# Head pairs on two PSUM banks, taps moved forward, squares added before the token sums, and x turned unscaled in a hybrid layer with attention and experts

## The reference, cut to what matters

```python
h = rms_norm(x, g_mix[i]); proj = h @ w_in[i]              # conv value, conv gate, q, k, v
conv_out = conformer_conv(c_val, c_gate, ...)              # 31 causal taps on 512 channels, LayerNorm, silu
attn = moba_attention(q, k, to_heads(v))                   # 8 heads of 64; at 512 tokens: causal over everything
mixed = concatenate([rms_norm(conv_out, beta_conv), rms_norm(attn, beta_attn)])
x = x + mixed @ w_out[i]
h = rms_norm(x, g_ffn[i])
g_logits = h @ w_group + b_group; e_all = h @ w_erouter + b_erouter   # 4 + 32 logits of each token
# top group, then its top 2 of 8 experts; the chosen experts' SwiGLU on each token, weighted
x = x + hier_moe(h, ...)
x = x + (p[i] @ w_ple_proj) * sigmoid(rms_norm(x, g_ple) @ w_ple_gate + b_ple_gate)
```

## Time and profile before

| | |
|---|---|
| median of 3 runs | 652.24 us |
| the profiled execution's own time | 651.7 us |
| its span | 649.8 us |
| PE busy | 551.8 us (85%) |
| DVE busy | 297.3 us (46%) |
| ACT busy | 185.7 us (29%) |
| POOL busy | 82.2 us (13%) |
| chain that ended last | PE 55%, DVE 19%, DMA 15%, ACT 7% |

### The profile page before, as it was taken

One profiled execution on the slowest core, in us unless ns is written; L12 is line 12 of the kernel. 1 busy time (PEld: TensorE's weight loads), 2 busy tenths in 40 slices (PEclk: granted clock), 3 DMA queues, 4 the chain that ended last, 5 costly groups with the idle time before them and its releaser, 6 DMA issues.

```text
span 649.8 us, 7753 instructions
## 1 busy us (share of the span) xinstructions
PE 551.8 (85%) x2628; PEld 322.9 (50%) x2629; DVE 297.3 (46%) x551; ACT 185.7 (29%) x348; POOL 82.2 (13%) x106
## 2 busy tenths in 40 slices
PE   1999999985779898897997889999999998729980
PEld 1788887753456687543332233333333332228870
DVE  3339868998872924474211111211121121175754
ACT  4831411346742432121101010110111010154554
POOL 0650000000000030002112012112211211000000
PEclk9999999996779989989999899999999999958995
DMA  8902102545004001664899998699899999265012
GB/s 342 384 3 72 67 9 58 219 144 211 1 0 195 1 1 66 266 283 168 323 418 419 421 421 348 235 419 385 335 417 422 368 421 419 119 259 210 2 43 86
DMA packets 34248, 145.86 MB, mean 224 GB/s; under 512 B 6576, under 2 KB 6832, under 8 KB 21808
## 3 DMA queue, kind: packets, MB, share of 16 engines
q1 hardware_dynamic: 27168, 133.70, 51.6%
q0 software_dynamic: 6480, 10.50, 4.4%
q10 hardware_dynamic: 576, 1.34, 0.5%
HBM read 142.90 MB, written 14.68 MB: 242 GB/s over the span
## 4 chain that ended last, share of the span: by engine, by line
PE 55%; DVE 19%; DMA 15%; ACT 7%; issue 2%; SPq 1%; POOL 0%; DVEq 0%; ACTq 0%; POOLq 0%
PE bank L1518 17%; DMA wring<-w_up_in 12%; PE bank L1266 10%; PE bank L1534 7%; DVE mix L888 6%; PE bank L1379 6%; PE bank L1563 2%; PE bank L1290 2%; DVE wring L946 2%; PE bank L1360 1%; PE bank L1497 1%; DMA c<-cst_in 1%; PE bank L1347 1%; PE bank L1444 1%; PE bank L1314 1%
## 5 line engine op out<-in xcount | busy, mean ns | idle before, releaser
L1518 PE MATMUL bank<-wring,arena 128*64 128x512 f32 x640 | 142.8, 599 | 13.7 <-SPq L506 12.0
L1518 PEld LDWEIGHTS bank<-wring,arena 128*64 128x64 f32 x640 | 46.2, 138 | 107.4 <-issue 90.1
L888 DVE SCALAR_TENSOR_TENSOR mix<-arena,pr,mix 128x512 f32<-128x512 f32 x120 | 81.5, 751 | 0.0
L1534 PE MATMUL bank<-wring,arena 128*64 128x512 f32 x320 | 73.1, 599 | 9.5 <-ACT arena L800 9.5
L1176 DVE TENSOR_TENSOR arena<-arena,bank 128x256 f32<-128x256 f32 x20 | 8.4, 422 | 148.7 <-ACT arena L797 148.7
L797 ACT ACTIVATE arena<-bank 128x256 f32<-128x256 f32 x20 | 7.7, 384 | 143.9 <-PE bank L1518 143.9
L1534 PEld LDWEIGHTS bank<-wring,arena 128*64 128x64 f32 x320 | 21.2, 136 | 48.5 <-issue 34.3
L1181 DVE COPY arena<-bank 128x512 f32<-128x512 f32 x20 | 13.8, 692 | 66.4 <-PE bank L1534 66.4
L1266 PE MATMUL bank<-hT_hi,win_hi 128*128 128x512 f32 x128 | 33.5, 398 | 1.5 <-DVE hT_lo L866 0.9
L803 ACT ACTIVATE arena<-bank 128x512 f32<-128x512 f32 x20 | 11.9, 597 | 75.8 <-PE bank L1534 75.8
L1266 PE MATMUL bank<-hT_lo,win_hi 128*128 128x512 f32 x128 | 31.6, 389 | 0.0
(11 more groups left out here) (203 smaller groups left out, 812.0 us busy)
## 6 DMA issues: line engine op xcount, KB each, us to landing
wring<-w_gate_in SPq DMA_DIRECT2D x32, 1024.0 KB, 10.4
wring<-w_up_in SPq DMA_DIRECT2D x32, 1024.0 KB, 12.7
wring<-w_down_in SPq DMA_DIRECT2D x32, 1024.0 KB, 15.6
wring<-w_in_in SPq DMA_DIRECT2D x5, 2048.0 KB, 19.1
wring<-w_out_in SPq DMA_DIRECT2D x2, 2048.0 KB, 8.0
wring<-y_d SPq DMA_DIRECT2D x8, 512.0 KB, 6.8
xs<-x_in SPq DMA_DIRECT2D x4, 512.0 KB, 7.5
xs<-x_in SPq DMA_DIRECT2D x1, 2048.0 KB, 8.0
```

Of the source, the lines that this page charges most:

```text
L888: ins = dve.scalar_tensor_tensor(out=mixc[:, mm, :], in0=u[:, mm, j:j + S], scalar=w, in1=mixc[:, mm, :], op0=ALU.mult, op1=ALU.add)
L1518: ins = pe.matmul(pb[2 + s][a * CAP:(a + 1) * CAP, :], xgT[:, s, k, a * CAP:(a + 1) * CAP], up_w(w, a)[:, :, k, :], start=(k == 0), stop=( ...
L1534: ins = pe.matmul(pb[6 + half][a * CAP:(a + 1) * CAP, :], hidT[:, s, k, a * CAP:(a + 1) * CAP], dn_w(w, a)[:, k, half * 512:(half + 1) * 5 ...
```

## The change

- **Banks.** Pairs of heads alternate between banks 6 and 7. "outa" uses five banks in turn and "outc" three; "h2" uses four; mean, var and the sums of squares move to banks 4 and 5.
- **Taps.** 71 in place of 66 taps stand before the attention, 13 of them ahead of the first turn of the rotation where 10 stood behind it; then seven each for four units, and one for each unit after that (two before). 13 are left after the last unit (6 before).
- **ACT.** probs_out goes ahead of attn_out, and the split of w_out's convolution half goes behind the loop.
- **Squares.** POOL adds the four tiles of the attention's squares, DVE those of the convolution; PE sums the one tile by token. The mean is made after the third "outa" group (before: second), conv_sq after the second "outc" group (before: first).
- **Router.** x is turned as it is, without the root. The gains are multiplied into wr once, on DVE. The logits are made with tokens on partitions, one tile after the other, and DVE multiplies by the root and adds a row of the bias, which was stored to memory and read back to all partitions by two small DMAs on SP's queue. ACT copies out one half of each turned tile, DVE the other. The rows' scaling for the gather remains, and for the last tile it stands in the middle of the router's chain on DVE. The DMA of wpp is issued ahead of the last "outc" group.

```diff
-GLU2, GLU3, TURN, EARLY = 20, 34, 54, 66
-TAPS_BY = (73, 80, 87, 94) + tuple(range(96, 120, 2))
+GLU2, GLU3, TURN, EARLY = 20, 34, 57, 71
+TAPS_BY = (78, 85, 92, 99) + tuple(range(100, 112))
...
-            banks.use(("attn", u // TT), 6)
-    banks.use("attn_sq", 7)
+            banks.use(("attn", u // TT), 6 + u // TT % 2)
+    banks.use("attn_sq", 4)
     for q in range(2 * TT):
-        banks.use(("outa", q), q % 4)
-    banks.use("mean", 4)
-    banks.use("var", 5)
+        banks.use(("outa", q), (0, 1, 2, 6, 7, 0, 1, 2)[q])
+    banks.use("mean", 5)
+    banks.use("var", 4)
     for q in range(2 * TT):
-        banks.use(("outc", q), q % 4)
-    banks.use("conv_sq", 7)
+        banks.use(("outc", q), q % 3)
+    banks.use("conv_sq", 5)
...
+            sp.wait_ge(prm_loaded, 32)
+            sp.dma_start(bias_d, pr[0:NR, Q_RB:Q_RB + 1]).then_inc(rbias_stored, 16)
             banks.wait_full(sp, ("v", TT - 1))
...
+            banks.wait_full(sp, ("outa", 2 * TT - 1))
+            sp.dma_start(wpp, ...).then_inc(ple_loaded, 16)
+            sp.wait_ge(rbias_stored, 16)
+            sp.wait_ge(osq_ready, CM)
+            sp.dma_start(bias_row, bias_d.rearrange("n a -> (a n)").partition_broadcast(P)).then_inc(rbias_loaded, 16)
             banks.wait_full(sp, ("outc", 2 * TT - 1))
-            sp.dma_start(wpp, ...).then_inc(ple_loaded, 16)
             sp.dma_start(pTs, ...).then_inc(ple_loaded, 16)
...
+            for m in range(CM):                          # POOL
+                banks.wait_emptied(pool, ("attn", m))
+                split_mix(1, mixa, m)
+                if m >= 1:
+                    pool.wait_ge(sqa_ready, m + 1)
+                    wait(pool, sq_added, m - 1)
+                    pool.tensor_tensor(sqa[:, 0, :], sqa[:, 0, :], sqa[:, m, :], ALU.add).then_inc(sq_added, 1)
...
-                if 9 <= u_ < 9 + CM:                     # ACT
-                    split_out(0, u_ - 9)
+                if u_ >= 2:
+                    probs_out(u_ - 2)
                 if u_ % TT == 3 and u_ > TT:
                     attn_out(u_ // TT - 1)
-                if u_ >= 2:
-                    probs_out(u_ - 2)
             attn_out(CM - 1)
+            act.wait_ge(woc_loaded, 16)
+            for m in range(CM):
+                split_out(0, m)
+            banks.wait_full(act, "attn_sq")
+            emptied(act.activation(gss[:, 1, :], bk("attn_sq")[:, 0:TT], ACT.Sqrt, ...), "attn_sq")
...
                 mean_root(1, t, junk)
+                banks.wait_full(act, ("h2", t, 1))
+                emptied(act.activation(hT[:, 4:8, t * P:(t + 1) * P], ..., ACT.Copy), ("h2", t, 1))
...
-            taps(GLU3 - 6, TURN - 10)                    # DVE
+            taps(GLU3 - 6, TURN)
             turn(0)
-            taps(TURN - 10, TURN)
+            dve.tensor_tensor(wr[:], wr[:], pr[:, Q_FFN:Q_FFN + DK]..., ALU.mult).then_inc(wr_scaled, 1)
             taps(TURN, EARLY)
...
-            for q in range(2):
+            for q in range(3):
                 add_scaled(("outa", q), 1, q)
...
+            for m in range(1, CM):
+                dve.wait_ge(osq_ready, m + 1)
+                wait(dve, csq_added, m - 1)
+                dve.tensor_tensor(sqc[:, 0, :], sqc[:, 0, :], sqc[:, m, :], ALU.add).then_inc(csq_added, 1)
...
             for q in range(2 * TT):
                 t, half = q // 2, q % 2
                 add_scaled(("outc", q), 0, q)
                 banks.wait_emptied(dve, ("outc", q))
                 if half == 0 and t >= 1:
+                    columns_out(t - 1)                   # one half of the tile, a plain copy
                     normal_rows(1, t - 1)
-                if half == 1 and t >= 2:
-                    columns_out("h2", t - 2, Q_FFN)
-            normal_rows(1, TT - 1)
-            columns_out("h2", TT - 2, Q_FFN)
-            columns_out("h2", TT - 1, Q_FFN)
+            columns_out(TT - 1)
+            inverse(1, TT - 1)
...
+            for t in range(TT):
+                ins = logits_out(t)     # lg = bank * rs + bias_row, scalar_tensor_tensor of 128x36
...
             dve.tensor_tensor(sm[:, 6, :], sm[:, 3, :], sm[:, 2, :], ALU.subtract).then_inc(exp_in, 1)
+            scaled_rows(1, TT - 1)
...
-                    for m in range(CM):                  # PE, channel_sum
-                        ins = pe.matmul(bk(name)[:, t:t + 1], src[:, m, ...], ones[:, 0:1], ...)
+                    ins = pe.matmul(bk(name)[:, t:t + 1], src[:, t * P:(t + 1) * P], ones[:, 0:1], start=True, stop=True)
...
-                if q == 0:
-                    attn_squares(CM - 1)
                 if q == 1:
+                    pe.wait_ge(sq_added, CM - 1)
+                    channel_sum("attn_sq", sqa[:, 0, :])
+                if q == 2:
                     pe.wait_ge(tap_done, CM * TAPS)
                     mean_of("mean", mixc)
...
-                if q == 0:
-                    pe.wait_ge(osq_ready, CM)
-                    channel_sum("conv_sq", sqc)
+                if q == 1:
+                    pe.wait_ge(csq_added, CM - 1)
+                    channel_sum("conv_sq", sqc[:, 0, :])
+                if half == 0 and t >= 1:
+                    turn_rows(t - 1)    # xs turned, after both outc groups of the tile were added
                 if half == 1 and t >= 1:
-                    turn_rows("h2", t - 1, TT)
+                    logits(t - 1)       # 8 matmuls: hT tile stationary, 36 columns of wr moving
+            turn_rows(TT - 1)
+            logits(TT - 1)
```

More of the change, by code:

```diff
@@ L1399, in _, with turn_rows, logits @@
                     attend(u_ - 3)
-                if u_ >= 2 * TT and u_ % TT == 0:
-                    attn_squares(u_ // TT - 2)
-            def turn_rows(kind, t, first):
-                pe.wait_ge(xn_ready, first + t + 1)
+            def turn_rows(t):
+                for half in range(2):
+                    banks.wait_emptied(pe, ("outc", 2 * t + half))
+                rows = xs[:, t, :].rearrange("p (n k) -> p k n", k=DK)
                 for kh in range(2):
-                    name = (kind, t, kh)
+                    name = ("h2", t, kh)
                     banks.wait_free(pe, name)
                     for k in range(4):
-                        ins = pe.transpose(bk(name)[:, k * P:(k + 1) * P], xn[:, t, 4 * kh + k, :], ident)
+                        ins = pe.transpose(bk(name)[:, k * P:(k + 1) * P], rows[:, 4 * kh + k, :], ident)
                     filled(ins, name)
+            def logits(t):
+                if t == 0:
+                    banks.wait_free(pe, "logit")
+                    pe.wait_ge(wr_scaled, 1)
+                for k in range(DK):
+                    if k % 4 == 0:
+                        banks.wait_emptied(pe, ("h2", t, k // 4))
+                    ins = pe.matmul(bk("logit")[:, t * NR:(t + 1) * NR], hT[:, k, t * P:(t + 1) * P], wr[:, k, :],
+                                    start=(k == 0), stop=(k == DK - 1))
+                if t == TT - 1:
+                    filled(ins, "logit")
             pe.wait_ge(wo_hi_ready[1], CM)
```

103 lines of the change are left out of this document (36 added, 67 removed).

## The result

| | before | after |
|---|---|---|
| median | 652.08 us (650.49 to 652.33, 4 runs) | 630.2 us (628.02 to 632.16, 4 runs) |
| ratio of the two | | 0.967 (0.963 to 0.971) |
| profiled execution, its span | 651.7, 649.8 | 628.79, 627.0 |
| PE busy | 551.8 | 538.7 |
| DVE busy | 297.3 | 304.1 |

The change made the kernel 3.3% faster. DVE is busier in total than before and yet has less of the chain: taps moved to places where PE does not wait for them.

The account below looks back on a forecast made before the run. PE paces up to 137 us, then a ring of engines waiting for one another until 200.5, then mostly PE. 15.5 - 1.9 + 9.7 - 1.7 = 21.6 off 651.7 gives 630.1, 630.6 us for the median; range 621 to 641 (own range 626 to 635).

Parts of the forecast that it names:

- Before 137: Attention's first four units, up to 137 us: PE paces them, so the earlier taps gain nothing there.
- The loop: From score(4) at 137 to the first outa matmul: that matmul at 185.0 in place of 200.5, gain 15.5 us.
- the allowance: In the loop from 137: 5 us added to the 38 for handshakes and PE partly at half clock.
- the prediction's sentence by that rule: Loop from 137: shorter gaps mean a fuller clock, the whole 5 us extra is not needed, sum 625.6.
- The new wait on the rotated rows: At unit 8 in the loop: score(8) waits for row DMAs until 150.7, could go at 148.4; 2.3 us, in the sum.
- Taps beside POOL: Before the last division, by the skill's rule: one POOL addition costs up to 1.27 us, loop's end 186.3, not 185.0.
- T to the end of the first outc group: From the first outa matmul (T): reciprocal at T+22.8, group's end at T+37.1 against T+35.2; net loss 1.9 us.
- To lg: From the end of the first outc group to the logits in lg: 33.1 us in place of 42.8, gain 9.7.
- Router: After the logits in lg: the "ple" products end late, so DVE has the count later; loss 1.7 us (0.8 to 3.5).
- The stream: Experts' stage: rival that the weight stream sets the end, gain only 14.3 us, total 637.9; chance 0.09.
- The ring: Loop from 137: rival that latency, not DVE's work, sets it, gain 7 to 10 us there, total 638; chance 0.16.
- The half clock: Output projection: rival of matmuls at half clock, whole gain gone from 26 fours on, all 48 give 671; chance 0.04.

Follow-up runs that it names:

- late_csq2: Changed kernel with DVE's three additions of the convolution's squares held back until POOL's last mixc_lo; 630.6 us, 0.965 of the kernel before.
- no_loop_taps2: Changed kernel with no taps in units 4 to 15, 25 left for the end; 633.3 us, 0.970 of the kernel before.
- two_queues2: Changed kernel with the second return of rotated rows issued half by SP's and half by POOL's queue; 629.51 us, 0.965 of the kernel before.
- one_bank: Changed kernel with all four pairs of heads on bank 6 again; 639.76 us, 0.981 of the kernel before.
- no_adds: Changed kernel without POOL's and DVE's additions of squares, PE summing all four tiles by token; 643.01 us, 0.985 of the kernel before.

## Why the prediction was right

The total was forecast at 630.6 and measured at 630.2, by the mechanism named: the bank's waits and the taps out of the ring, at the price of a later mean. That it came so near is partly luck. Against the forecast the five terms were off by -3.1, +2.1, +0.5, -0.9 and +0.2 us, together -1.2 in the profiled execution, and the 0.4 of the median is a tenth of what the four executions spread over.

- **Before 137: nothing gained.** Right: PE works 26.58 of 26.90 us at the full clock, as in the first row.
- **The loop.** The way was right and the allowance too large. The walk through the units gave 38 us, 35 of DVE's work and 3 of its waiting, and 5 were added, in all 43; it took 39.4, of which DVE worked 38.0 and stood still 1.4. So DVE's work was put 3 too low, 2.2 of it what POOL took (1.07 on a tap, 1.17 on a division), and waits and allowance, 8 together, were put 6.6 too high. PE's mean clock was 0.95 and not 0.76; between 0.91 and 0.95 it made no difference, since late_csq2 had 0.91 and a loop as long. The Trainium skill (TensorE: Matmul & The Clock Gate, "HAM oscillation — how this bites in real kernels") says that long gaps in PE's work bring the clock down, and with the bank's gaps gone it stayed up, as the prediction's sentence by that rule had it; the 625.6 of that sentence was not reached, since the later terms took back what the loop gave beyond the forecast. From the last division to T it was 5.5, not 5. The premise that DVE's work bounds the loop was half right: it took 37.97 of 39.40 us, but without its taps the ring is at most 1 us faster (no_loop_taps2). A forecast that took more work off DVE would have failed.
- **The new wait on the rotated rows.** Forecast 2.3 us, score(8) at 150.7; measured 2.60 and 151.4. That it costs was wrong: two_queues2 took 1.9 of it away, T moved 0.15, and the loop's length 0.1.
- **Taps beside POOL.** The rule of the Trainium skill (SBUF — State Buffer, "Who interferes with whom") that a DVE instruction with two SBUF inputs and a POOL instruction that reads SBUF block each other holds here: 1.82 us for a tap beside a POOL subtraction, 12.83 and 10.74 for 13 taps beside four and two, and POOL's own operation goes from 1.27 to 1.72. I left it out of the sum, and the sentence by that rule priced one wait of up to 1.27 in the loop where there were two, of 1.07 and 1.17. They are inside the 39.4. Behind the loop the blocking took 4.2 of the 6 us by which the taps' end was to lead the mean. They ended at 189.2, 2.6 before the mean, so this cost nothing, but with less cover it would have.
- **T to the end of the first outc group.** The reciprocal at T+22.8 was forecast to the tenth (204.74). The mis-sized term is what follows: mixc_lo ended at T+37.3, not T+36.0, because DVE's adds of the squares run beside it (6.32 for 5.06; late_csq2 takes them away and has 4.98 again), and the group then ended 1.9 us after it, not 1.1, at the low clock (in one_bank, without the dip, it is 1.1). I had read 5.06 from a row with nothing beside it, and had named the dip only among the rivals. Loss 4.0 for 1.9.
- **To lg.** 33.6 for 33.1. The logits cost less than I took, three times 1.71 on the chain and once 1.98 (251.85), 7.1 for 8.0; the seven groups more, 20.8 for 19.0, some 1.2 of it the dip that ran into the second group (3.93 for 2.72).
- **Router.** 0.8 for 1.7. The four "ple" products end at T+78.8, as forecast (T+78 to T+79), but lg comes 2.6 us later after T than forecast, at T+72.8, and so DVE has chosen (260.78) just when they end. What remains is the scaling of 1.16 in DVE's chain.
- **The rivals.** The stream did not set the end: the second slot's load was issued at 249.2 (forecast 249.5) and the whole 22.8 us arrived, DMA share 0.91. The ring kept one kind of its waits (6.4 us on ACT's copies, L738) but not the bank's. The half clock took about four fours of matmuls of the output projection, not 26.

## What to carry to other kernels

A ring of engines has several limits that lie close together: removing the longest wait (7 us for the bank) and unloading the busiest engine (8.5 for the taps) both paid, and unloading it further paid nothing, because the way round was nearly as long. Move work off the critical stretch, but look at what runs beside it in its new place: an addition that hid perfectly on DVE stretched the POOL operation that PE waited for. Read steps of 1 to 3 us from their place in the trace, since a later stage whose clock dips can swallow them in the total.

## What the runs showed of the hardware

- DVE and POOL block each other both ways: a tap of 0.75 us takes 1.82 beside a POOL operation of 1.27, and POOL's takes 1.72 when DVE was first. Each POOL operation cost a run of taps 1.05 to 1.07 us.
- A wait of PE of 2.4 us was followed by the low clock in six profiles of nine; with 14 extra matmuls in the gap it was not, in one profile. 32 matmuls of one column each were followed by it as well, with no idle time of PE in them or behind them (3.74 us in no_adds, then 2.06 for four matmuls; 3.46 in the kernel before, and 1.91 for four at 240.09).
- 16 float32 matmuls with 36 columns moving took 1.87 to 1.98 us, nearly as much as 16 with 68 (2.00): between these widths the columns hardly set the time.
- The same experts' stage took 273.4 to 278.2 us, longer where its granted clock was 0.97 than where it was 0.99.
